# Expert scatter as two rounded passes with a 0/1 matrix turned from the gather's; gate weight in the output's copy; a full 128-row sample tile in the gather

## The reference

```python
def moe(x, router_w, wg, wu, wd):
    xt = x.reshape(B * T, D)
    logits = (xt @ router_w).astype(jnp.float32)
    top_v, top_i = lax.top_k(logits, TOP_K)              # TOP_K = 2
    gates = jax.nn.softmax(top_v, axis=-1)
    combine = jnp.sum(jax.nn.one_hot(top_i, N_EXPERTS) * gates[..., None], axis=1)
    out = jnp.zeros_like(xt)
    for e in range(N_EXPERTS):                           # 8 experts, hidden width 1408
        out = out + combine[:, e:e + 1] * swiglu(xt, wg[e], wu[e], wd[e])
    return out

def swiglu(x, wg, wu, wd):
    return (jax.nn.silu(x @ wg) * (x @ wu)) @ wd
```

## Time and profile before

| | |
|---|---|
| median of three timed runs | 1230.55 us (1226.32 to 1233.48) |
| the profiled execution: its time / its span | 1220.12 us / 1218.3 us |
| PE busy | 1111.4 us, 91% |
| DVE busy | 795.8 us, 65% |
| ACT busy | 645.7 us, 53% |
| POOL busy | 15.0 us, 1% |
| expert stage with its first gather | from 728.7 to about 1192 us of the span |

### The profile page before, as it was taken

One profiled execution on the slowest core, in us unless ns is written; L12 is line 12 of the kernel. 1 busy time (PEld: TensorE's weight loads), 2 busy tenths in 40 slices (PEclk: granted clock), 3 DMA queues, 4 the chain that ended last, 5 costly groups with the idle time before them and its releaser, 6 DMA issues.

```text
span 1218.3 us, 19957 instructions
## 1 busy us (share of the span) xinstructions
PE 1111.4 (91%) x7698; PEld 1027.6 (84%) x7698; DVE 795.8 (65%) x1125; ACT 645.7 (53%) x864; POOL 15.0 (1%) x34
## 2 busy tenths in 40 slices
PE   6998996599999998998966789999999999999995
PEld 5998983399999998998943778998989898989984
DVE  5689641275655555787621464886888688868883
ACT  5675541255433445675421334775767476666762
POOL 0001000000000000010000000000000000000000
PEclk9999998699999999999988876999999999999998
DMA  8443457845555554544647333995989598959861
GB/s 326 155 157 126 164 199 297 313 147 181 185 178 187 174 190 132 171 142 150 223 164 291 137 150 117 347 360 207 346 302 372 192 365 289 361 202 362 306 261 38
DMA packets 64276, 273.00 MB, mean 224 GB/s; under 512 B 7328, under 2 KB 7584, under 8 KB 63552
## 3 DMA queue, kind: packets, MB, share of 16 engines
q1 hardware_dynamic: 62352, 264.33, 61.2%
q0 software_dynamic: 1408, 7.12, 1.6%
q10 hardware_dynamic: 432, 0.38, 0.1%
HBM read 265.83 MB, written 5.98 MB: 223 GB/s over the span
## 4 chain that ended last, share of the span: by engine, by line
PE 71%; DVE 14%; ACT 6%; DMA 4%; issue 3%; SPq 1%; DVEq 0%; ACTq 0%
PE bank L590 10%; PE bank L587 10%; PE bank L592 10%; PE bank L591 10%; PE bank L588 10%; PE bank L589 10%; DMA ring<-dense 4%; DVE wl L1370 3%; PE bank L848 2%; ACT wh L993 2%; DVE rstd L1365 2%; PE bank L615 1%; DVE wl L1621 1%; DVE sq L1381 1%; PE bank L748 1%
## 5 line engine op out<-in xcount | busy, mean ns | idle before, releaser
L1621 DVE TENSOR_TENSOR wl<-ring,wh 128x1408 fp32r<-128x1408 f32 x192 | 310.2, 1624 | 60.4 <-ACT wh L1237 60.2
L1370 DVE TENSOR_TENSOR wl<-ring,wh 128x1024 fp32r<-128x1024 f32 x170 | 206.9, 1223 | 215.7 <-ACT wh L993 215.3
L1237 ACT ACTIVATE wh<-ring 128x1408 fp32r<-128x1408 f32 x189 | 261.0, 1381 | 85.9 <-PE bank L592 85.6
L587 PE MATMUL bank<-xh,wh 128*128 128x264 f32 x928 | 271.6, 293 | 19.0 <-DVE xl L1386 14.7
L993 ACT ACTIVATE wh<-ring 128x1024 fp32r<-128x1024 f32 x170 | 178.8, 1056 | 190.0 <-PE bank L589 143.4
L588 PE MATMUL bank<-xl,wh 128*128 128x264 f32 x928 | 267.3, 288 | 0.0
L589 PE MATMUL bank<-xh,wl 128*128 128x264 f32 x928 | 266.6, 287 | 0.0
L591 PE MATMUL bank<-wh,xl 128*128 128x352 f32 (+4 forms) x736 | 243.9, 331 | 0.0
L587 PEld LDWEIGHTS bank<-xh,wh 128*128 128x128 f32 x928 | 178.6, 192 | 25.6 <-issue 21.4
L588 PEld LDWEIGHTS bank<-xl,wh 128*128 128x128 f32 x928 | 179.1, 193 | 0.0
L589 PEld LDWEIGHTS bank<-xh,wl 128*128 128x128 f32 x928 | 178.3, 192 | 0.0
(11 more groups left out here) (217 smaller groups left out, 1370.1 us busy)
## 6 DMA issues: line engine op xcount, KB each, us to landing
ring<-experts SPq DMA_DIRECT2D x192, 704.0 KB, 5.9
ring<-dense SPq DMA_DIRECT2D x234, 512.0 KB, 3.8
o_k<-kv POOLq DMA_DIRECT2D x2, 1024.0 KB, 4.4
o_v<-kv POOLq DMA_DIRECT2D x2, 1024.0 KB, 7.7
x<-xT SPq DMA_DIRECT2D x2, 528.0 KB, 4.9
o_y<-sq SPq DMA_DIRECT2D x4, 264.0 KB, 2.1
gatew<-gate_w POOLq DMA_DIRECT2D x2, 512.0 KB, 8.3
mem<-memT SPq DMA_DIRECT2D x1, 1024.0 KB, 13.3
```

Of the source, the lines that this page charges most:

```text
L587: mm(out, s_hi, m_hi, start=start, stop=False)
L1237: A(wh[:, jj % NBUF, :], eraw(jj % ESLOTS), ACT.Copy).then_inc(ehi_ready, 1)
L1370: V.tensor_tensor(wl[:, k % NBUF, 0:UNIT], raw(u), wh[:, k % NBUF, 0:UNIT].bitcast(F32), ALU.subtract)\
L1621: V.tensor_tensor(wl[:, jj % NBUF, :], eraw(jj % ESLOTS), wh[:, jj % NBUF, :].bitcast(F32), ALU.subtract)\
```

## The change

- The scatter takes two passes of f32r matmuls, with the output's high part `eoh` and low part `eol`, against a 0/1 matrix. `eo`, `wsel` and DVE's `scatter_matrix` go.
- The 0/1 matrix is turned from `gsel` itself: S is now three f32r matmuls of `gsel` with a rounded identity, and three more, of two columns, with the gate weights' parts (`gcol`), which give each slot's gate. S moves from behind T0 of the next expert to behind group 1 of the same expert, and exists for all eight there; the one in the tail goes.
- ACT copies S into one half of `scat` and then the two gate columns with a running sum, so that `gate` holds the slot's gate weight. Both come between the high parts of units 9 and 10.
- ACT's copy of D0 and D1 is scaled with `gate` and rounded (`eoh`); DVE makes `eol` with one operation on 128x512 (bank times gate minus `eoh`), for D0 behind the low part of unit 22 and for D1 behind that of unit 26, which is unit 2 of the next expert.
- `gather_matrix(p + 1)` moves from the start of the a block to the b block, between the low parts of units 10 and 11, behind a wait for S; `gate_columns(p + 1)`, two small operations, follows it.
- The gather's third tile has 128 rows: POOL clears that tile once, before the tokens are copied into 8 of its rows.

```diff
-    HIDDEN = ["G0", "U0", "G1", "U1", "G2", "U2", "T0", "S", "G3", "U3", "T1"]
+    HIDDEN = ["G0", "U0", "G1", "U1", "S", "G2", "U2", "T0", "G3", "U3", "T1"]
...
-                            slots = gsel[0:rows, t, :, :].rearrange("p b s -> p (b s)")
-                            mm(out, tokh[0:rows, t, f0:f0 + P], slots, start=(t == 0), stop=False)
-                            i = mm(out, tokl[0:rows, t, f0:f0 + P], slots, start=False, stop=(t == 2))
+                            slots = gsel[:, t, :, :].rearrange("p b s -> p (b s)")
+                            mm(out, tokh[:, t, f0:f0 + P], slots, start=(t == 0), stop=False)
+                            i = mm(out, tokl[:, t, f0:f0 + P], slots, start=False, stop=(t == 2))
...
-                pe.wait_ge(wsel_ready, v + 1)
+                pe.wait_ge(gcol_lo_ready, p + 1)
                 for t, (t0, rows) in enumerate(TOK):
-                    i = nc.tensor.transpose(b[:, t0:t0 + rows], wsel[0:rows, t, :], ident[0:rows, 0:rows])
+                    mm(b[:, t0:t0 + rows], gsel[:, t, side, :], identr[:, 0:rows], start=True, stop=True)
+                for t in range(3):
+                    i = mm(b[:, T:T + 2], gsel[:, t, side, :], gcol[:, t, side, :], start=(t == 0), stop=(t == 2))
                 full(i, n)
...
-                    full(mm(b[:, 0:T], eo[:, c * P:(c + 1) * P], scat, start=True, stop=True), n)
+                    mm(b[:, 0:T], eoh[:, c * P:(c + 1) * P], s, start=True, stop=False)
+                    full(mm(b[:, 0:T], eol[:, c * P:(c + 1) * P], s, start=False, stop=True), n)
...
                 group(1)
+                turn_scatter(p, side, num)
                 group(2)
                 turn_hidden(num, 0)
-                if not first:
-                    turn_scatter(v - 1, num)
                 group(3)
...
-                read(A(scat, bank(n)[:, 0:T], ACT.Copy), n)
+                A(scat[:, side * T:(side + 1) * T], bank(n)[:, 0:T], ACT.Copy).then_inc(gate_ready, 1)
+                read(A(gate2[:, side, :], bank(n)[:, T:T + 2], ACT.Copy, accum_out=gate[:, side:side + 1]), n)
...
+                upto(10)
+                scattered(side, num)
                 upto(12)
...
-                    read(A(eo[:, u * 512:(u + 1) * 512], bank(n)[:, :], ACT.Copy), n)
+                    A(eoh[:, u * 512:(u + 1) * 512], bank(n)[:, :], ACT.Copy, scale=gate[:, side:side + 1]).then_inc(eoh_ready, 1)
...
+            def gate_columns(p):
+
+                gates = wcol[:, :, bass.ds(2 * p, 2)]
+                V.tensor_copy(gcol[:, :, :, 0], gates).then_inc(gcol_ready, 1)
+                dve.wait_ge(gcol_ready, p + 1)
+                V.tensor_tensor(gcol[:, :, :, 1], gates, gcol[:, :, :, 0].bitcast(F32), ALU.subtract).then_inc(gcol_lo_ready, 1)
...
-                if side == 0 and not last:
-
-                    wait_full(dve, *before("X3"))
-                    gather_matrix(p + 1)
                 upto(6)
                 hidden(0)
                 upto(10)
                 hidden(1)
+                upto(11)
+                if side == 1 and not last:
+
+                    wait_full(dve, *num("S"))
+                    gather_matrix(p + 1)
+                    gate_columns(p + 1)
                 upto(14)
...
-                scatter_matrix(v)
-                upto(27)
+                upto(23)
+                wait_read(dve, *num("S"))
+                for u in range(2):
+                    n, more = num(f"D{u}")
+                    dve.wait_ge(eoh_ready, 2 * v + u + 1)
+                    cols = slice(u * 512, (u + 1) * 512)
+                    read(V.scalar_tensor_tensor(out=eol[:, cols], in0=bank(n)[:, :], scalar=gate[:, side:side + 1],
+                                                in1=eoh[:, cols].bitcast(F32), op0=ALU.mult, op1=ALU.subtract), n)
+                    upto(27)
...
+            wait_full(pool, tiles[("kn", DEPTH - 1, 1)])
+            G.memset(tokh[:, 2, :].bitcast(F32), 0.0).then_inc(tail_zeroed, 1)
+            G.memset(tokl[:, 2, :].bitcast(F32), 0.0).then_inc(tail_zeroed, 1)
```

More of the change, by code:

```diff
@@ L186, in trunk_kernel @@
     MID = ["a" + x for x in HIDDEN + COMBINE + OUTPUT] + ["b" + x for x in HIDDEN + COMBINE + GATHER + OUTPUT]
-    FIRST = ["a" + x for x in HIDDEN + OUTPUT if x != "S"] + [x for x in MID if x[0] == "b"]
+    FIRST = ["a" + x for x in HIDDEN + OUTPUT] + [x for x in MID if x[0] == "b"]
     LAST = [x for x in MID if x[1] != "X"]
-    TAIL = ["S"] + COMBINE
+    TAIL = COMBINE
     assert len(MID) == 48
@@ L246, in trunk_kernel @@
         rstd = sb("rstd", [P, 2, T])
+        shared = nc.sbuf_base
         mem = sb("mem", [P, KC, NM])
@@ L249, in trunk_kernel @@
         gatew = sb("gatew", [P, 2, RC, P])
+        room = nc.sbuf_base - shared
         rw = sb("rw", [P, KC, NE])
@@ L316, in trunk_kernel @@
         at[0] = 0
-        wsel = take(3 * CAP).rearrange("p (t s) -> p t s", t=3)
         esg = take(2 * GW).rearrange("p (i n) -> p i n", i=2)
@@ L324, in trunk_kernel, with reuse @@
         gsel = xh[:, FEC * CAP:(FEC + 6) * CAP].rearrange("p (t b s) -> p t b s", t=3, b=2)
-        eo = kv[:, 0:D]
-        scat = kv[:, D:D + T]
+        after_mixers = [0]
+        def reuse(name, shape):
+            size = 4 * shape[1]
+            assert after_mixers[0] + size <= room
+            after_mixers[0] += size
+            return nc.alloc_sbuf_tensor_at(name, shape, F32R, offset=shared + after_mixers[0] - size)
+        eoh = reuse("expert_out_hi", [P, D])
+        eol = reuse("expert_out_lo", [P, D])
+        scat = reuse("scatter", [P, 2 * T])
+        identr = reuse("identity", [P, P])
+        gcol = reuse("gate_columns", [P, 12]).rearrange("p (t b k) -> p t b k", t=3, b=2)
         rt = kv[:, 2 * D:3 * D]
@@ L344, in trunk_kernel @@
         second = rt[:, 309:333].rearrange("p (t e) -> p t e", t=3)
+        gate2 = rt[:, 340:344].rearrange("p (b k) -> p b k", b=2)
+        gate = rt[:, 344:346]
         def per_token(a):
@@ L414, in trunk_kernel @@
         mask_ready = sem("mask_ready")
+        tail_zeroed = sem("sample_token_tile_zeroed")
         route_ready = sem("route_ready")
         gsel_ready = sem("gather_matrix_ready")
-        wsel_ready = sem("scatter_matrix_ready")
+        gcol_ready = sem("gate_column_hi_ready")
+        gcol_lo_ready = sem("gate_column_lo_ready")
+        ident_ready = sem("rounded_identity_ready")
+        gate_ready = sem("slot_gates_ready")
+        eoh_ready = sem("expert_out_hi_ready")
         x_final = sem("x_final")
@@ L913, in expert @@
                 if not first:
-                    scatter(num, before)
+                    scatter(num, before, 1 - side)
                 if side == 1 and not last:
@@ L947, in run_pass @@
                 pair(p1, ps.last, ps.earlier(p1), last=True)
-                turn_scatter(2 * p1 + 1, ps.after)
-                scatter(ps.after, block_of(ps.last, "b"))
+                scatter(ps.after, block_of(ps.last, "b"), 1)
             for t in range(3):
@@ L953, in _ @@
                     wait_read(pe, tiles[("tk", l, t, hp)])
+            pe.wait_ge(ident_ready, 1)
             run_pass(main)
@@ L1221, in _ @@
             first_highs(0)
+            act.wait_ge(tail_zeroed, 2)
             for t, (t0, rows) in enumerate(TOK):
@@ L1226, in _ @@
                     A(tokh[0:rows, t, hp * 512:(hp + 1) * 512], bank(n)[0:rows, :], ACT.Copy).then_inc(oh_ready, 1)
+            A(identr[:, :], ident, ACT.Copy).then_inc(ident_ready, 1)
             act.wait_ge(lmax_ready, 1)
@@ L1280, in expert @@
                 turned(num, 0)
-                if not first:
-                    scattered(num)
                 upto(16)
@@ L1290, in expert @@
                 upto(23)
+                wait_read(act, *num("S"))
                 for u in range(2):
@@ L1309, in run_pass @@
                 pair(p1, ps.last, last=True)
-                scattered(ps.after)
             run_pass(main)
@@ L1680, in gather_matrix @@
                 i.then_inc(gsel_ready, 1)
-            def scatter_matrix(v):
-                for t in range(3):
-                    i = V.tensor_scalar(wsel[:, t, :], iota, pcol[:, t, bass.ds(v, 1)], wcol[:, t, bass.ds(v, 1)],
-                                        ALU.is_equal, ALU.mult)
-                i.then_inc(wsel_ready, 1)
+            def gate_columns(p):
[3 more added lines that the diff above has]
+                V.tensor_tensor(gcol[:, :, :, 1], gates, gcol[:, :, :, 0].bitcast(F32), ALU.subtract).then_inc(gcol_lo_ready, 1)
             def combine(num):
@@ L1760, in run_pass @@
                     gather_matrix(p0)
+                    gate_columns(p0)
                     for j in range(NBUF):
@@ L1781, in _ @@
                 step(V.tensor_tensor(wts[:, :, b, :], oh, second, ALU.add))
+            after(chain[0])
+            gate_columns(0)
             run_pass(main)
```

9 lines of the change are left out of this document (5 added, 4 removed).

## The result

The changed kernel took 1208.28 us (median of four runs, 1205.46 to 1211.25) beside 1228.43 for the kernel before (four runs, 1220.62 to 1233.48): ratio 0.984, 95% interval 0.980 to 0.988. It is 20 us faster; the forecast was 1222.6 us, and the measured time lies 6 us under the lower end of its 80% range. Its profiled execution took 1205.46 us, span 1203.7, 14.6 us under the span of the first trace of before.

What follows compares the result with a forecast made beforehand. PE's list of matmuls was taken to bound the expert stage, with DVE's chain ending last at the scatter. Terms summed to -7.9 us: 1220.12 to 1212.2, plus 10.4 for timed runs gave 1222.6 us; 80% range 1214 to 1231.

Steps and rivals of the forecast that it cites:

- the median of the three runs, 1230.55, lies 10.4 above it, and I add that.: Whole kernel: timed median taken as 10.4 us above the profiled 1220.12 us, added to the predicted 1212.2 us.
- I take three falls in seven: +5.0: Seven waits behind the scatter, about 2.4 us each: three drop the clock, +5.0 us; bounds 0 and 11.6.
- a sign of being wrong: Between 750 and 1190 us, three low-clock stretches of some 3.3 us were expected; none, or longer ones, would refute the forecast.
- The first rival: No fall of the clock at the seven waits behind the scatter: -12.9 in sum, 1217.6 us; chance 0.25.
- The fifth rival: Scatter's saving lands in seven blocks because additions start with C0, no falls: -25.5 in sum, 1205 us; chance 0.04.
- Gathers in the loop: Three loop gathers, with 128 rows in the third tile, run at dense pace, 5.5 us for 8.74: -9.7 us.
- First gather and group 0: First gather goes from 15.0 to 8.0 us as the clock rises within it; group 0 gains too: -9.4 us.
- Scatter: Two-pass scatter shortens PE by 1.8 us, but DVE's chain ends last: direct gain 0, bound -1.8 a block.
- S: S behind group 1, six matmuls at T0's pace, 0.66 us for 0.46: +2.1 us over eight experts.
- The copies of S on ACT: ACT's copies between units 9 and 10 make unit 10 late by 0 to 0.1 us: +0.5 in eight experts.
- Gather matrix: In three b blocks, gather matrix and gate columns on DVE make unit 11's low part 1.2 us late: +3.6 us.
- Tail: Shorter last scatter offset by the output's low part on DVE, about 0.69 us, with S gone: 0.

Runs made afterwards that it cites:

- the second trace of before: The kernel before, unchanged, profiled once more: 1234.9 us, span 1233.1.
- the high pass alone: The changed kernel with only the high pass of the scatter (8 matmuls, output's low part left out): 1216.98 us, ratio 0.988 to the kernel before.
- the kernel with 8 rows: The changed kernel with only the gather's third tile back at 8 rows: 1249.26 us, ratio 1.014 to the kernel before.
- the scatter made twice: The changed kernel with each of the scatter's eight products made twice (32 matmuls): 1208.25 us, ratio 0.981 to the kernel before.
- the additions first: The changed kernel with DVE's eight additions ahead of the low part of unit 18: 1196.39 us; the same order on the kernel before with full rows: 1197.42 us.
- The full rows alone: The kernel before with only the gather's third tile made 128 rows: 1204.57 us, ratio 0.979.
- the gather matrix in pieces: The changed kernel with DVE's additions ahead of unit 18's low part and the gather matrix dealt out behind units 10, 11 and 12: 1193.37 us, ratio 0.969.

## Why the prediction was wrong

Its main mechanism held, that all of the gain is the full rows'; two steps failed, both on the clock.

**"the median of the three runs, 1230.55, lies 10.4 above it, and I add that."** This is the step that failed most. The 10.4 us were no constant of the timing. Judged by the second trace of before and by the clocks of its timed runs, they were one or two falls of the clock in the loop's gathers, 5.8 us each, and up to 3 us of other differences; the first trace happens to have no such fall. No trace of a kernel with full rows in the loop has a fall there, except the one with the high pass alone and, once, behind the last wait, the second one of the changed kernel; and the changed kernel's median stands only 2.8 us above its profiled run. The 14.6 us of span and one fall make the measured 20.

**"I take three falls in seven: +5.0."** The two traces of the changed kernel have none and one; none was what the prediction itself had named as a sign of being wrong. The wait was sized rightly: it came in two parts, of 1.9 to 2.0 us together by PE's idle times and 2.35 from start to start, where 2.4 were forecast. What failed is the step from the wait to the fall. The number of falls is not settled by the wait alone: 2.8 us gave five falls of seven, and the same 2 us gave seven of seven in the kernel with 8 rows, also behind T2, where nothing near the wait differs from the changed kernel. What sets that is open. A rule of the Trainium skill (TensorE: Matmul & The Clock Gate, section "HAM oscillation — how this bites in real kernels") has the clock fall on idle gaps longer than these; the falls behind waits of 0.7, 2 and 2.8 us do not agree with it. The first rival, with no falls, had the right sign of this term: 1217.6 with the same wrong offset, and 1207 without it. The fifth rival's 1205 us also lies near the measured time, but by luck: its mechanism, a saving of the scatter that lands, is refuted by the 4.87 us from T1 to the gather and by the scatter made twice.

The other terms, in spans:

- *Gathers in the loop*: -9.7 forecast, 3 x (8.74 - 5.76) = -8.9 measured.
- *First gather and group 0*: -9.4. The stretch from the gather's first matmul to group 0's fell from 16.75 us to 9.89, -6.9, and group 0 ran at 1.00; but 0.60 us of that went into a wait for a low part at 746.83, since DVE was now the later: about -8.7 in all. The clock rose in the gather, as the step said.
- *Scatter*: 0, and 0 it was; the scatter twice and the additions first show that DVE's order ended last. The bound of -1.8 a block lies in that order: 12 us.
- *S*: +2.1; 0.58 us each, 0.12 more than before in seven and 0.58 in one, +1.4. The estimate of 0.21 from the isolated gaps in the Trainium skill (the same page, section "Back-to-back issue gap") does not agree with these rows; T0's pace did better.
- *The copies of S on ACT*: +0.5; no wait for unit 10 shows in the loop.
- *Gather matrix*: +3.6; waits of 0.64, 0.73 and 0.73, +2.1. The gate columns took 0.3 and not 0.4, and the low parts of units 11 to 13 ran on without a pause. Besides, the 0.2 us at the start of two a blocks, which I took as nothing, went.
- *Tail*: 0; from its first scatter matmul to the end it was 22.9 us (1195.41 to 1218.3) and became 21.2 (1182.49 to 1203.7), -1.7; but from the last matmul of D1 to that point it became 0.8 longer, since the wait for the output's low part, 1.76 us, took the place of S and of a wait of 0.60: -0.9.

These make -15.4 with the 0.4 of the a blocks; the span fell by 14.6, so some 0.8 us, 0.1 an expert, are not put down to a row.

The prediction had -19.1 us for the full rows and +11.2 for everything else. The full rows alone are indeed faster than the change: by the traces they give -16.9, and its other parts, with the order of DVE's queue as it was, cost 2 to 4 us. With the additions first the two-pass scatter is no slower than the old one (464.6 and 465.7 us from the first gather to the end; 1196.4 and 1197.4 us, on different chips), and with the gather matrix in pieces some 4 us ahead.

## What to carry to other kernels

Ask why the profiled execution differs from the timed runs before adding the difference as a constant: here the mean clock of each run told that it was a second behaviour, which the change removes. Compare the starts of instructions, not only the idle times printed beside them: the waits of 0.6 to 0.7 us here were worth 0.8 to 1.1. A shorter step on the bounding engine gains nothing while another engine's queue ends later; look for the instruction in that queue which nobody waits for yet, and move it behind. Matmuls of few rows among full ones cost time of their own (8.74 us a gather against 5.76), and in these traces a low clock lasted longer among them.

## What the runs showed of the hardware

Two things I had not expected. Behind a wait of 0.7 us the clock could fall to 1.2 GHz when a gather with 8-row matmuls followed (two of three in one trace, none of three in another), and without the wait no run showed it; ahead of the full-row gather the same wait left the clock at 1.00 in the trace. And leaving out half of the scatter's matmuls made the kernel 9 us slower, because five of the seven longer waits, 2.8 us in three parts, came with a fall, four of them of about 6.8 us.
